# Two transformer blocks on one core: VectorE's order at the end of the first block's layers, remainders signalled one by one, and five small moves

## What is computed

```python
        ffn = jnp.einsum('bsf,fd->bsd', hidden, w_ffn_out[l])
        x = layer_norm(DN_ALPHA * x + ffn, ln2_g[l], ln2_b[l])
```

```python
        h = rms_norm_2(x, attn_norm_g[i])
        proj = h @ w_in[i]
        ...
        x = x + (jax.nn.silu(gate) * up) @ w_down[i]
```

## Time and profile before

| | |
|---|---|
| median of three runs | 1495.82 us |
| profiled execution | 1495.67 us |
| its span | 1494.2 us |
| TensorE (PE) busy | 1465.1 us, 98% |
| VectorE (DVE) busy | 1003.1 us, 67% |
| ScalarE (ACT) busy | 784.9 us, 53% |
| GpSimd (POOL) busy | 64.1 us, 4% |
| mean granted TensorE clock | 1.00 |

### The profile page before, as it was taken

The page is one execution under the profiler, slowest core; times in us unless marked ns, Lnnn a source line. Parts: engine busy times, 40 slices in busy tenths (PEclk is TensorE's granted clock), DMA queues, the critical chain, the costliest instruction groups (busy, mean ns, idle before and its releaser), DMA issues.

```text
span 1494.2 us, 18393 instructions
## 1 busy us (share of the span) xinstructions
PE 1465.1 (98%) x7191; PEld 1203.8 (81%) x7191; DVE 1003.1 (67%) x1349; ACT 784.9 (53%) x1124; POOL 64.1 (4%) x100
## 2 busy tenths in 40 slices
PE   7999999999999999999999999999999999999998
PEld 5788887888887787887878887788888888888887
DVE  5656885864556655885865555877766668777765
ACT  3565644443443555745344333686655557756553
POOL 2000000000001000000010000210000012000000
PEclk9999999999999999999999999999999999999999
DMA  8544643575564535552765664436555644455551
GB/s 317 188 155 131 237 170 124 171 241 182 184 209 156 203 116 158 183 169 85 234 214 174 201 190 169 142 115 195 184 182 169 197 151 158 155 166 187 170 188 66
DMA packets 167317, 260.99 MB, mean 175 GB/s; under 512 B 8768, under 2 KB 106720, under 8 KB 166720
## 3 DMA queue, kind: packets, MB, share of 16 engines
q1 hardware_dynamic: 166048, 252.03, 51.6%
q0 software_dynamic: 896, 6.74, 1.2%
q10 hardware_dynamic: 288, 1.05, 0.2%
HBM read 258.74 MB, written 1.05 MB: 174 GB/s over the span
## 4 chain that ended last, share of the span: by engine, by line
PE 82%; DVE 10%; ACT 4%; issue 2%; POOL 1%; DMA 1%; SPq 0%; DVEq 0%; ACTq 0%
PE ps L384 15%; PE ps L388 15%; PE ps L386 15%; PE ps L457 10%; PE ps L459 9%; PE ps L458 9%; DVE wlo L1500 3%; ACT whi L1069 2%; PE ps L1001 1%; PE ps L511 1%; PE ps L534 1%; PE ps L414 1%; DVE x L1519 1%; DVE x L1517 1%; PE ps L524 1%
## 5 line engine op out<-in xcount | busy, mean ns | idle before, releaser
L1500 DVE TENSOR_TENSOR wlo<-raw,whi 128x2048 fp32r<-128x2048 f32 (+1 forms) x238 | 528.2, 2229 | 275.0 <-ACT whi L1069 274.4
L1069 ACT ACTIVATE whi<-raw 128x2048 fp32r<-128x2048 f32 (+1 forms) x238 | 441.7, 1865 | 204.7 <-PE ps L388 124.9
L384 PE MATMUL ps<-whi,xTh 128*128 128x512 f32 x704 | 277.4, 394 | 0.0
L388 PE MATMUL ps<-whi,xTl 128*128 128x512 f32 x704 | 274.4, 390 | 0.0
L386 PE MATMUL ps<-wlo,xTh 128*128 128x512 f32 x704 | 274.1, 389 | 0.0
L457 PE MATMUL ps<-whi,xTh 128*128 128x512 f32 (+3 forms) x640 | 251.1, 392 | 7.4 <-DVE xTl L1538 3.4
L459 PE MATMUL ps<-whi,xTl 128*128 128x512 f32 (+3 forms) x640 | 242.1, 378 | 0.0
L458 PE MATMUL ps<-wlo,xTh 128*128 128x512 f32 (+3 forms) x640 | 241.4, 377 | 0.0
L388 PEld LDWEIGHTS ps<-whi,xTl 128*128 128x128 f32 x704 | 132.1, 188 | 27.9
L384 PEld LDWEIGHTS ps<-whi,xTh 128*128 128x128 f32 x704 | 132.2, 188 | 27.6 <-issue 0.8
L386 PEld LDWEIGHTS ps<-wlo,xTh 128*128 128x128 f32 x704 | 132.3, 188 | 26.4
(11 more groups left out here) (185 smaller groups left out, 1635.2 us busy)
## 6 DMA issues: line engine op xcount, KB each, us to landing
raw<-in_w_in SPq DMA_DIRECT2D x124, 512.0 KB, 4.6
raw<-in_w_ffn_in SPq DMA_DIRECT2D x88, 512.0 KB, 4.8
raw<-in_w_up SPq DMA_DIRECT2D x88, 512.0 KB, 4.9
raw<-in_w_ffn_out SPq DMA_DIRECT2D x44, 512.0 KB, 4.4
raw<-in_w_down SPq DMA_DIRECT2D x44, 512.0 KB, 4.6
raw<-in_w_branch SPq DMA_DIRECT2D x24, 512.0 KB, 4.6
raw<-in_w_out SPq DMA_DIRECT2D x16, 512.0 KB, 4.5
raw<-in_w_o SPq DMA_DIRECT2D x16, 512.0 KB, 4.5
```

Of the source, the lines that this page charges most:

```text
L384: PE.matmul(o, ah, hi[:, j, b], start=first and kt == 0, stop=False)
L388: mm = PE.matmul(o, al, hi[:, j, b], start=False, stop=last and j == c - 1 and i == len(kts) - 1)
L1069: AC.activation(m.whi[:, i % SPLIT, 0:w], m.raw[:, slot, 0:w], ACT.Copy).then_inc(s.w_hi, 1)
L1500: DV.tensor_tensor(m.wlo[:, i % SPLIT, 0:w], m.raw[:, slot, 0:w], m.whi[:, i % SPLIT, 0:w].bitcast(F32), ALU.subtract).then_inc(s.w_lo, 1)
```

## The change

- **End of a layer of block 1** (both layers), VectorE: `add_down(0)` and `stats(0)` stand ahead of `split_to(later + 1)`, and `hidden_half(1)` stands behind it and behind the first mean subtraction. `apply(0)` is taken apart into `center` and `scale_up`. `add_down(1)` moves behind the second quarter's remainder. TensorE: the first quarter's transposes stand ahead of the last down product's first column block instead of its second.
- **Remainders with gains**: each of the four instructions raises `turn_lo`, and TensorE waits for one column block at a time (60 further waits).
- **End of block 2's first layer**, TensorE: the second quarter's transposes move behind the last down product.
- **Convolution**: the first `conv_turn` moves from the third to the fourth column block.
- **Neighbourhood attention**, ScalarE: at `g == 4` one `split_to` moves behind both copies of probabilities.
- **Start**: the first half of x comes as two DMAs of 128x512, one on SyncE's and one on ScalarE's queue, and the second weight piece is loaded ahead of the second half of x.

```diff
-    SP.dma_start(m.x[:, 0, :], t["x"][0, 0:P, :]).then_inc(s.x_in, 16)
+    SP.dma_start(m.x[:, 0, 0:512], t["x"][0, 0:P, 0:512]).then_inc(s.x_in, 16)
...
         load_piece(w1[:, 0:4, 0:512], 4, 512)
+        load_piece(w1[:, 4:8, 0:512], 4, 512)
         if not L:
             SP.dma_start(m.x[:, 1, :], t["x"][0, P:S, :]).then_inc(s.x_in2, 16)
-        load_piece(w1[:, 4:8, 0:512], 4, 512)
...
     def x_ready(th, kt):
-        if kt in (0, 4):
-            PE.wait_ge(s.turn_lo, x_lo[th, kt // 4])
+        count, remainders = x_lo[th, kt // 4]
+        if remainders == 4:
+            PE.wait_ge(s.turn_lo, count - 3 + kt % 4)
+        elif kt in (0, 4):
+            PE.wait_ge(s.turn_lo, count)
...
         def first_x_turn(th, kt):
-            if kt == 1:
-                turn_x(0, 0)
+            if kt == 0:
+                turn_x(0, 0, remainders=last_use)
...
         def down_turn(th, kt):
             if kt == 1:
-                for n4 in range(2):
-                    turn_x(0, n4)
+                turn_x(0, 0, remainders=4)
...
         def first_conv_turn(th, kt):
-            if (th, kt) == (0, 2):
+            if (th, kt) == (0, 3):
...
             down(c, 1, down_turn if c == NSTEP - 1 and L + 1 < DEPTH else None)
+        if L + 1 < DEPTH:
+            turn_x(0, 1, remainders=4)
...
+    AC.dma_start(m.x[:, 0, 512:D], t["x"][0, 0:P, 512:D]).then_inc(s.x_in1, 16)
...
-            catch(1, L, "na", g, 2, ahead=SPLIT - (g == 4))
+            catch(1, L, "na", g, 2, ahead=0 if g == 4 else SPLIT)
...
-            a = DV.scalar_tensor_tensor(out=m.xTl[:, kt, o], ...
+            DV.scalar_tensor_tensor(out=m.xTl[:, kt, o], ...
-        a.then_inc(s.turn_lo, 1)
+                                    op1=ALU.subtract).then_inc(s.turn_lo, 1)
...
         hidden_half(0)
         h_lo(slice(0, P), 2)
-        split_to(later + 1)
         add_down(0, (1, L, "dn", NSTEP - 1))
-        hidden_half(1)
         for n4 in range(2):
             stats(0, n4)
+        split_to(later + 1)
+        DV.wait_ge(s.vec, 32 * (L + 2))
+        center(0, 0)
+        hidden_half(1)
+        scale_up(0, 0)
         h_lo(slice(P, S), 2)
-        DV.wait_ge(s.vec, 32 * (L + 2))
-        apply(0)
+        center(0, 1)
+        scale_up(0, 1)
...
         split_to(later + 2)
-        add_down(1, (1, L, "dn", NSTEP - 1))
         if L + 1 < DEPTH:
             turn_lo_quarter(0, 1)
         else:
             turn_lo_gains(0, 1, 16)
+        add_down(1, (1, L, "dn", NSTEP - 1))
```

More of the change, by code:

```diff
@@ L52 @@
     "free0", "free1", "free2",
-    "x_in", "x_in2", "par", "vec", "lay", "gate_b", "gate_b2", "ln_in", "stored",
+    "x_in", "x_in1", "x_in2", "par", "vec", "lay", "gate_b", "gate_b2", "ln_in", "stored",
     "init",
@@ L408, in gate_cols, with turn_quarter @@
         return m.gate[:, th, kt * P:(kt + 1) * P]
-    def turn_quarter(src, th, n4):
+    def turn_quarter(src, th, n4, remainders=1):
         bank = ps[:, 4 + 2 * th + n4, :].rearrange("p (k s) -> p k s", k=4)
@@ L415, in turn_quarter, with turn_x @@
         mm.then_inc(s.turned, 1)
-        return n.up("turn_lo")
-    def turn_x(th, n4, ready=None):
+        return n.up("turn_lo", remainders)
+    def turn_x(th, n4, ready=None, remainders=1):
         if ready:
@@ L424, in turn_x @@
             PE.wait_ge(s.normed, n.up("normed"))
-        x_lo[th, n4] = turn_quarter(x_cols, th, n4)
+        x_lo[th, n4] = turn_quarter(x_cols, th, n4, remainders), remainders
     def x_ready(th, kt):
-        if kt in (0, 4):
-            PE.wait_ge(s.turn_lo, x_lo[th, kt // 4])
+        count, remainders = x_lo[th, kt // 4]
[3 more added lines that the diff above has]
+            PE.wait_ge(s.turn_lo, count)
     x_lo = {}
@@ L840, in tensor_program @@
         up(end, (1,), (1,))
+        last_use = 1 if L + 1 < DEPTH else 4
         def last_half_turn(th, kt):
@@ L852, in tensor_program @@
         down(end, (1,), first_x_turn)
-        turn_x(0, 1)
+        turn_x(0, 1, remainders=last_use)
     for L in range(DEPTH):
@@ L858, in x_ready_turn @@
             if kt in ((1, 2), (5, 6))[L == 0]:
-                turn_x(1, kt - (1, 5)[L == 0])
+                turn_x(1, kt - (1, 5)[L == 0], remainders=4)
         for i, (name, kts, width, th, before) in enumerate((("q", (4, 4), 512, 0, x_ready), ("k", (8,), 256, 0, x_ready_turn),
@@ L986, in out_turn @@
             if kt in (1, 2):
-                turn_x(0, kt - 1, (2, L, "a", kt - 1))
+                turn_x(0, kt - 1, (2, L, "a", kt - 1), 4)
         for i, (j, th, before) in enumerate(((0, 0, outputs_ready), (1, 0, None), (0, 1, out_turn), (1, 1, None))):
@@ L1021, in up_turn @@
                 n4 = kt // 2 - 1
-                turn_x(1, n4, (2, L, "a", n4))
+                turn_x(1, n4, (2, L, "a", n4), 4)
             x_ready(th, kt)
@@ L1510, in stats, with center, scale_up, apply @@
             DV.bn_aggr(m.mv[:, th, :], m.bn[:, th, :, :].rearrange("p a b -> p (a b)")).then_inc(s.moments, 1)
-    def apply(th, n4s=(0, 1)):
-        if 0 in n4s:
+    def center(th, n4):
+        if n4 == 0:
             DV.wait_ge(s.rstd, n.up("rstd"))
[L1515 to L1520, removed]
-                                    op1=ALU.add).then_inc(s.normed, 1)
+        c = slice(n4 * 512, n4 * 512 + 512)
+        then(DV.scalar_tensor_tensor(out=m.x[:, th, c], in0=m.x[:, th, c], scalar=m.mv[:, th, 0:1], in1=m.vec[:, c],
+                                     op0=ALU.subtract, op1=ALU.mult))
+    def scale_up(th, n4):
+        c = slice(n4 * 512, n4 * 512 + 512)
+        DV.scalar_tensor_tensor(out=m.x[:, th, c], in0=m.x[:, th, c], scalar=m.small[:, th:th + 1],
+                                in1=m.vec[:, D + n4 * 512:D + n4 * 512 + 512], op0=ALU.mult,
+                                op1=ALU.add).then_inc(s.normed, 1)
+    def apply(th):
+        for n4 in range(2):
+            center(th, n4)
+            scale_up(th, n4)
     def turn_lo_quarter(th, n4, scale=1.0):
@@ L1742, in vector_program @@
     DV.wait_ge(s.x_in, 16)
-    for n4 in range(2):
-        stats(0, n4)
+    stats(0, 0)
+    DV.wait_ge(s.x_in1, 16)
+    stats(0, 1)
     for L in range(DEPTH):
```

5 lines of the change are left out of this document (2 added, 3 removed).

## The result

The changed kernel takes **1499.01 us** (median of 12 runs, 1498.38 to 1500.3), the one before 1495.80 (12 runs, 1495.46 to 1496.29). The ratio is 1.0022 with a 95% interval of 1.0014 to 1.0031: 3.2 us slower. The profiled execution took 1499.6 us, its span is 1498.2, and the mean granted clock is 0.997 where it was 1.00.

What follows compares the result with a forecast made beforehand. TensorE bounds the kernel, busy 1465.1 of 1494.2 us. Terms 1.3 + 0.95 − 0.4 − 0.6 − 0.3 + 0.6 + 0 − 0.45 = +1.1 us on 1495.67, so 1496.8, forecast as median 1496.9; range 1494.0 to 1500.0.

Steps and rivals of the forecast that it cites:

- the 0.2% that the text gave 0.20: Whole kernel: chance 0.20 of being slower by over 0.2% (3.0 us), which needs over 1498.8 us.
- the chain at the end of block 1's layers: VectorE's new order makes `hidden` 3.4 us late; half 1's first product +1.3 us, second layer's k product +0.95.
- third rival: Block 1's layer ends: `hidden` isn't late, named waits go and nothing replaces them; −6.8 us, 1489.0; chance 0.05.
- The first rival: TensorE's clock falls at `hidden`'s transposes, 2.25 us each; one layer 1499.1, both 1501.4; chance 0.14.
- GpSimd's hold: Block 1's layer ends: GpSimd's `rstd` waits until VectorE's weight remainder ends; without it each layer comes 0.8 us earlier.
- The start: Program start: smaller first DMA and earlier second weight piece remove waits, −0.45 us; bounds −1.0 and +1.5.
- The fear for `ln_b`: Program start: `ln_g` and `ln_b` queue behind half of x and may hold back the first norm; bound +1.5 us.
- Between block 2's layers: TensorE's 0.80 us wait at 1214.95 goes, and k is released earlier: −0.6 us, bounds −0.9 and 0.
- The convolution: `conv_turn` one column block later makes VectorE wait: +0.3 us per layer, +0.6; bounds 0 and 0.68 each.
- ScalarE's move: Neighbourhood attention at `g == 4`: one rounding behind the copies fills no TensorE idle time; 0 us, bounds 0.4 and −0.1.

Runs made afterwards that it cites:

- e4: Changed kernel with 26 identity transposes on TensorE in the idle stretch ahead of `hidden`'s transposes: 1496.41 us, ratio 1.0007.
- e2: Kernel before with only VectorE's new order at the end of block 1's layers: 1502.07 us, ratio 1.0046.
- e5: Changed kernel with `hidden` of half 1 made right behind the aggregate, ahead of the 128x2048 weight remainder: 1496.21 us, ratio 1.0004.
- e3: Changed kernel with `hidden` of half 1 ahead of the mean subtraction, still behind the 128x2048 remainder: 1493.77 us, ratio 0.9987.
- e8: Kernel before with the changed start alone (x's first half as two DMAs, order of loads): 1495.32 us beside 1495.88, ratio 0.9997.
- e6: e3 with the third 128x2048 remainder moved ahead of half 1's statistics: 1494.40 us.
- e7: As e6, with the third remainder also ahead of `add_down(1)`: 1494.99 us.
- e1: Changed kernel with VectorE's old order at the end of block 1's layers: 1494.82 us, ratio 0.9994.
- e9: e3 with 12 identity transposes on TensorE ahead of `hidden`'s transposes: 1493.46 us, ratio 0.9985.
- e11: e3 with the first `conv_turn` back at the third column block: 1493.03 us, ratio 0.9982.
- e10: e1 with 16 identity transposes on TensorE ahead of x's first transposes: 1494.08 us, ratio 0.9988.
- e12: e9 and e11 together, plus 14 identity transposes ahead of the k product behind the second layer: 1492.90 us, ratio 0.9983.

## Why the prediction was right or wrong

The time lay in the range (1494.0 to 1500.0), 2.1 us above the forecast, and just past the 0.2% that the text gave 0.20. That it lay in the range is in part luck: without the falls the forecast holds almost to the number (e4), and the falls, to which the text gave 0.14, added 2.6 us (the changed kernel's median against e4's), just about what the range had room for, since it reached up to one layer's fall.

**Right: the chain at the end of block 1's layers.** `hidden`'s transposes waited 3.41 and 3.42 us for VectorE's `gate`, where 3.5 was forecast. GpSimd was held for 2.12 us and the subtraction waited 0.80 for it, against 0.8 taken. With TensorE kept busy (e4) the two layers cost +1.41 and +0.41 us, against +1.3 and +0.55; and e4's median, 1496.41, is 0.5 us from the forecast of 1496.9. The waits at 471.70 and 937.95 went as said; the one at half 1's first product is 0.84 us where some 0.9 was forecast, and the one at the k product 1.82. The prediction overlooked the waits of 0.99 us at 477.92 and 0.79 at 933.46 in the kernel before. Its sum doesn't suffer, as it follows VectorE's work to half 1's first product and not TensorE's waits on the way; but they are part of how 3.4 us shrink to 1.3, and its third rival, which adds up the waits that go, leaves them out. (A slip without effect: 1214.95 less 0.80 is 1214.15, not 1214.05.)

**Wrong: the clock.** The forecast's step "the longest that the rows show is 1.48, and no clock fell there" was sound, but the chance of 0.14 made of it was not. The argument against, that the stretch is "hardly longer than the estimate's own error", compared it with nothing that was measured. The first rival is what happened. Its time for one layer, 1499.1, is the measured 1499.0, though by another sum, so that this hit is chance too: three falls that cost 3.7 us together in the profiled execution. It priced a fall at 2.25 us and had one or two; the profile shows 3.4 us at the lower level each time, so 1.7 us of work lost, part of it in time that would have been waited, and a third fall that no rival had, behind a stretch of 1.8 us. And it took the length of a stretch to decide, which e2 contradicts.
The Trainium skill, TensorE: Matmul & The Clock Gate, section "Why this matters for your kernels", warns against idle gaps between bursts of matmuls. The trace agrees that such gaps can bring the lower level back, 3.4 us ones in both layers of the changed kernel; in other profiles stretches of 1.8 to 2.75 us did it too, and some of 3.4 us didn't (e2).

**Right: GpSimd's hold as VectorE's doing.** GpSimd's first instruction took 2.12 us beside a remainder, whose two inputs lie in SBUF. It took 0.19 in the kernel before at 469.17, beside `h_lo`, which reads one input from PSUM (VectorE, 469.00 to 469.37), and 0.19 beside nothing in e5. The Trainium skill's rule in SBUF — State Buffer, "Who interferes with whom", gave the same. What a free GpSimd alone would be worth isn't settled: in e5 it was free, but the clock fell; in e3 it was held, and `hidden` filled the time.

**Sizes.** The start gave −0.56 by the medians of e8 and −0.43 in e8's profile, and −0.78 in the changed kernel's, which is one draw from −0.18 to −0.96; the forecast was −0.45. The fear for `ln_b` was right in that it ate x's whole gain, but less by coming later than by having been nearly as late before. Between block 2's layers −0.62 against −0.6. The convolution 0.15 us per layer where 0.3 was taken: the whole stretch from the finer wait to the convolution came out at −0.07 instead of +0.15. ScalarE's move was run in no version alone, but from 98.90 to the end of the first layer's last product of half 0 nothing is lost or won: the row at 462.91 stands at 462.13, −0.78 like the one at 98.12. That fits the forecast's 0.

**Wrong: the third rival's idea of what `hidden` in time is worth.** It gave −6.8 us. e5 had `hidden` in time and came out at 1496.21, and no version here came under 1492.9. With the remainder in VectorE's row behind `add_down(0)`, TensorE waited for that row's end in every version here, if not for `hidden` then for what stands behind it (e6 and e7 only moved the wait to half 1's x).

What stays open is what decides whether a given stretch brings a fall. Idle stretches of 3.41 and 3.42 us did in one profile and did not in another (e2); 2.26 did and 2.28 did not in the same one (e1); those of 1.74 and 1.75 never did in the profiles here (eight cases). At one and the same place, the k product behind the second layer, a stretch of 1.97 us did (e9) and those of 1.95, 1.96 and 1.98 (e11, e3, e4) didn't.

## What to carry to other kernels

When TensorE is the bound and an order is changed on another engine, add up not only how late TensorE resumes but how long it stands still in one piece: the same lateness cost 1.4 us with the engine kept busy and 2.95 us without. A large instruction that used to run while its engine waited for TensorE (here a 2.2 us remainder) isn't free any more once it stands behind the wait; and if the small thing that TensorE waits for can go ahead of the step that waits for GpSimd, the exchange of two lines is the whole repair. Where the idle stretch can't be removed, products of the identity into a free bank are worth a try: in the profiles here no fall follows a stretch that they filled (e4, e9, e10, e12), and e4 was 2.6 us faster than the changed kernel by them.

## What the runs showed of the hardware

- An idle stretch of 3.4 us on TensorE isn't needed for the clock to fall to its lower level: it did behind 1.81, 1.82, 1.97, 2.15, 2.26 and 2.75 us, each time for 3.4 us, starting 0.1 to 1.5 us after the matmuls had resumed. Equal stretches in other executions passed at the upper level. The runs of such a kernel scatter more: over 1.9 us in the changed one and 4.0 in e2. The kernel before spread over 0.4 to 1.3 us beside the different versions.
- With 26 identity transposes in 3.00 us (0.12 us each) in the stretch, e4's profile shows the upper level behind it in both layers.
- At the program's start nine identity products take 2.18 us, twice what they take later, and yet the granted clock of the changed kernel's first 24 us reads 1.00. The forecast had read the lower level there from the durations; the clock column doesn't show it.

```profile
0.00:24.00 24.00, 14.81 (x69) 1.00 0.92 316
```

- The first of GpSimd's two instructions for this norm (L289, 128x1) took 0.19 us, or 2.12 beside one of VectorE's 128x2048 remainders, which is until that remainder ended; no length between appears in these profiles.
